# Narrow experts turn their activations by two half-width products, and experts two to eight are taken in another order

## The reference

```python
logits = einsum('bsd,de->bse', h, router_w) + router_b
top_vals, top_idx = lax.top_k(logits, 2)
top_w = softmax(top_vals)
combine = sum(one_hot(top_idx, 8) * top_w[..., None], axis=-2)
y = 0
for e in range(8):
    y = y + combine[..., e:e+1] * ((silu(h @ w_gate[e]) * (h @ w_up[e])) @ w_down[e])
x = x + gate_f * y
```

## Time and profile before

| | |
|---|---|
| median of three runs | 2416.67 us |
| lowest and highest | 2416.08, 2418.52 us |
| span of the profiled execution | 2415.4 us |
| TensorE busy | 2368.4 us, 98% of the span |
| VectorE busy | 935.5 us, 39% |
| ScalarE busy | 365.3 us, 15% |
| memory read | 614.69 MB |
| experts' stage, from the first expert's first product | 1464 us to the end |

### The profile page before, as it was taken

One profiled execution on the slowest core, in us unless ns is written; L12 is line 12 of the kernel. 1 busy time (PEld: TensorE's weight loads), 2 busy tenths in 40 slices (PEclk: granted clock), 3 DMA queues, 4 the chain that ended last, 5 costly groups with the idle time before them and its releaser, 6 DMA issues.

```text
span 2415.4 us, 30120 instructions
## 1 busy us (share of the span) xinstructions
PE 2368.4 (98%) x12002; PEld 1576.6 (65%) x12003; DVE 935.5 (39%) x1962; ACT 365.3 (15%) x988; POOL 55.4 (2%) x110
## 2 busy tenths in 40 slices
PE   9999999999999999999999999999999999999997
PEld 8956466669665666676788756699754445444553
DVE  4565233255564356755687462100211011101021
ACT  2254010012351100011000112100110010101111
POOL 0000000000000000000000000000000000000000
PEclk9999999999999999999999999999999999999999
DMA  7422343444322777454577469974999599958997
GB/s 277 149 111 97 113 173 141 152 177 167 128 81 94 270 297 299 194 194 192 227 302 308 167 247 394 424 289 186 375 422 419 206 381 421 425 231 358 417 426 295
DMA packets 78990, 617.61 MB, mean 256 GB/s; under 512 B 5984, under 2 KB 6112, under 8 KB 39184
## 3 DMA queue, kind: packets, MB, share of 16 engines
q1 hardware_dynamic: 73920, 558.39, 58.2%
q0 software_dynamic: 4656, 56.47, 5.6%
q10 hardware_dynamic: 288, 0.90, 0.1%
HBM read 614.69 MB, written 1.05 MB: 255 GB/s over the span
## 4 chain that ended last, share of the span: by engine, by line
PE 92%; DMA 4%; DVE 2%; ACT 1%; issue 1%; SPq 0%; POOL 0%; DVEq 0%; POOLq 0%; ACTq 0%
PE S L2972 9%; PE T L2592 9%; PE S L2974 8%; PE G L2331 6%; PE G L2608 5%; PE G L2986 4%; PE G L2988 4%; PE G L2363 3%; PE G L2546 3%; PE G L2871 3%; DMA big<-in_moe_pack 3%; PE S L2852 2%; PE G L2674 2%; PE T L3038 2%; PE G L2558 2%; PE G L3065 2%
## 5 line engine op out<-in xcount | busy, mean ns | idle before, releaser
L2186 DVE TENSOR_TENSOR turns<-S,turns 128x128 f32<-128x128 f32 (+2 forms) x105 | 35.5, 338 | 664.6 <-ACT turns L1280 664.6
L2972 PE MATMUL S<-big,hT 128*64 128x256 f32 x2240 | 272.1, 386 | 17.1 <-DMA big<-in_moe_pack 10.2
L2972 PEld LDWEIGHTS S<-big,hT 128*64 128x64 f32 x2240 | 157.1, 138 | 126.6 <-issue 44.2
L2592 PE MATMUL T<-hT,big 128*128 128x256 f32 x960 | 217.1, 379 | 1.1 <-ACT big L1168 1.1
L2592 PEld LDWEIGHTS T<-hT,big 128*128 128x128 f32 x960 | 182.1, 190 | 49.5 <-issue 27.7
L2974 PE MATMUL S<-big,hT 128*128 128x512 f32 x448 | 201.3, 593 | 0.3
L2974 PEld LDWEIGHTS S<-big,hT 128*128 128x128 f32 x448 | 82.8, 190 | 94.7 <-issue 94.7
L2363 PE MATMUL G<-big,hT 128*128 128x384 f32 x320 | 109.0, 490 | 0.8 <-ACT big L1058 0.8
L1285 ACT ACTIVATE pT<-T 128x128 f32<-128x128 f32 (+1 forms) x98 | 30.2, 308 | 518.9 <-PE T L2951 518.9
L2331 PE MATMUL G<-big 128*128 128x186 f32 (+1 forms) x536 | 91.8, 322 | 0.0
L2331 PEld LDWEIGHTS G<-big 128*128 128x128 f32 x536 | 86.6, 190 | 0.2
(11 more groups left out here) (500 smaller groups left out, 3494.6 us busy)
## 6 DMA issues: line engine op xcount, KB each, us to landing
big<-in_moe_pack SPq DMA_DIRECT2D x112, 2048.0 KB, 12.8
big<-in_moe_pack SPq DMA_DIRECT2D x72, 1024.0 KB, 10.0
big<-in_w_ff SPq DMA_DIRECT2D x32, 2048.0 KB, 8.0
big<-in_ada_pack POOLq DMA_DIRECT2D x24, 2048.0 KB, 12.2
big<-in_ffn_pack SPq DMA_DIRECT2D x11, 3072.0 KB, 12.7
big<-in_gate_pack SPq DMA_DIRECT2D x16, 1536.0 KB, 6.4
consts<-in_moe_pack SPq DMA_DIRECT2D x24, 1024.0 KB, 11.4
big<-in_proj_pack SPq DMA_DIRECT2D x15, 1488.0 KB, 6.4
```

The lines of the kernel that those rows point to most:

```text
L2592: ins = mm(up_bank(c, f), w[:, k, f * P:(f + 1) * P], hT[:, k, :], start=(k == 0), stop=(k == KD - 1))
L2972: ins = mm(S[s % 2][f * FEW:(f + 1) * FEW, 0:SEQ], hTe[:, k, 0:FEW], wt[:, k, f * SEQ:(f + 1) * SEQ], start=(k == 0), stop=(k == KD - 1))
```

## The change

`RANK_AT` becomes [0, 6, 0, 5, 1, 4, 2, 3]: after expert 0 come the fewest, the most, the second fewest, the second most and so on. Only the table changes; the code that each engine runs for a width stays where it is, and the table's row is an input.

In `turn_hidden` a narrow expert no longer transposes. It issues two ordinary products, each with 64 hidden channels of the activations as the stationary operand and the identity as the moving one, to PSUM partitions 0 to 63 and 64 to 127. The values land in the same places as before.

```diff
-RANK_AT = [0] + [(i - 1) // 2 if i % 2 else EXPERTS - 1 - i // 2 for i in range(1, EXPERTS)]
+RANK_AT = [0] + [TURNS - 1 - (i - 1) // 2 if i % 2 else i // 2 - 1 for i in range(1, EXPERTS)]
...
                     def turn_hidden(e, s, w):
 
                         pe.wait_ge(ehid_ok.sem, e * ESTEPS + (s + 3))
-                        for f in range(1 if few(w) else FT):
-                            ins = pe.transpose(T[0][:, s % 2 * SEQ + f * P:s % 2 * SEQ + (f + 1) * P], emsg[:, s % 2, SEQ + f * P:SEQ + (f + 1) * P], ident[:])
+                        for f in range(FT):
+                            if few(w):
+                                ins = mm(T[0][f * FEW:(f + 1) * FEW, s % 2 * SEQ:s % 2 * SEQ + P], emsg[:, s % 2, SEQ + f * FEW:SEQ + (f + 1) * FEW], ident[:], start=True, stop=True)
+                            else:
+                                ins = pe.transpose(T[0][:, s % 2 * SEQ + f * P:s % 2 * SEQ + (f + 1) * P], emsg[:, s % 2, SEQ + f * P:SEQ + (f + 1) * P], ident[:])
                         ins.then_inc(eh_turned.sem, 1)
```

## The result

| | before | changed |
|---|---|---|
| median, 20 runs each | 2418.8 us | 2424.2 us |
| lowest and highest | 2416.08, 2422.14 | 2418.64, 2431.19 |
| span of the profiled execution | 2415.4 | 2423.0 |

The ratio is 1.0023, with a 95% interval of 1.0017 to 1.0029: slower by 5.4 us, where 6.2 us less were forecast. The time lies 7 us above the end of the range, 2417.

The account below looks back on a forecast made before the run. TensorE, busy 98%, was taken as the bound, with DMA binding two neighbouring narrow experts. Terms -0.4 - 7.4 - 0.2 + 1.8 gave -6.2 us: span 2409.2, median 2410.5, range 2407 to 2417.

Parts of the forecast that it names:

- the order of the experts: Expert sequence: same seven width transitions, so the same pauses; the DMA-bound pair moves to turns 1 and 2; -0.4 us.
- The third: Rival: the 0.30 us around the transpose stay, turn 0.52 us, step from 5.64 us; +5.7 us, 2422.4; chance 0.10.
- The first rival's slower form: Turn's two halves don't run side by side, turn 0.44 us: +3.3 us, 2420.0; whole rival's chance 0.22.
- The turn within a step: Narrow experts: two products take 0.22 us where the transpose cost 0.41; 39 turns gain, -7.4 us; step 5.39 us.
- The turn of the last step: Between 128-wide gathers: 0.57 us with two switches instead of 0.11, +0.46 in four narrow experts, +1.8 us.
- A narrow expert followed by a narrow one: Narrow experts outside the DMA-bound pair: three, at -2.0 us each by the prediction's term.
- The DMA-bound pair: Two neighbouring narrow experts, moved from turns 7, 8 to 1, 2: stall 11.2 us against 10.2, at 425 GB/s.
- the 1650 named as the sign of a wrong term: Wide expert, forecast to start near 1647; a start beyond 1650 would make the order's term wrong.
- the first 12 pieces: Weights at the new pair's start: 18.9 MB in at 1464, leaving 69.2 MB to load from 1467.9 on.
- ScalarE's copy: Behind the turn, before `down`: slack of 0.31 us shrinks to about 0.1; the cover holds, but is thin.
- The order's -0.4: Term for the new expert order: last narrow expert done at 2405.8 against 2406.2; bounds +2.2 and -11.6 us.
- the late pair: Old order's two neighbouring narrow experts at turns 7 and 8, the last waiting 10.2 us for weights.

Follow-up runs that it names:

- before_pad84: Kernel before, plus 84 never-run instructions between TensorE's narrow and full bodies: 2432.61 us, ratio 1.0049 to the kernel before.
- order_only: Kernel before with only the new table of turns, the turn staying one transpose: 2420.09 us against 2419.77, ratio 0.9998.
- After_ahead128: Changed kernel plus 128 never-run instructions ahead of all TensorE expert code: 2400.83 us in one run; timed again 2403.63, ratio 0.9930 to the kernel before.

## Why the prediction was wrong

The step that failed is the one on the order of the experts: "So the 3.46 us in which TensorE waits for nothing shown between a full and a narrow expert, with the slow 5.36 and 5.26 us first group behind it ..., are paid twice in both". They are paid twice, but the price is 8.96 and 9.31, which is +11.35 us. I had counted the transitions and read their price as a property of the transition. It is one of where the code lies. That the code for each width stays where it is, as I wrote of the table, is true of the table alone: the two products make the narrow body longer and move the full body by 84 instructions. `before_pad84` shows the price with no change at all. No rival of mine had this either. The third, of a turn that keeps its 0.30 us, said 2422.4 and so comes nearest to 2424.2, by luck: its mark, a step of 5.64 or more, is absent, for the step is 5.39. The first rival's slower form, a turn of 0.44, is absent as well: the turn takes 0.22.

The other steps, by their own terms:

- The turn within a step was right: 0.22 us and 0.86 behind it. The saving is 0.19 us in 39 turns.
- The turn of the last step was right: 0.37 and 0.20 more behind it, the 0.57 that was forecast.
- A narrow expert followed by a narrow one takes 82.8 us in the changed kernel (84.9 with the old turn, in `order_only`), -2.0 as the sum had it.
- The DMA-bound pair: the wide expert starts at 1649.93, just below the 1650 named as the sign of a wrong term. Less the 3.8 us of the late start that is 1646.1, where 1647.1 was forecast; the stall is 11.4 us where 11 to 16 was expected, and the rate 425 GB/s, as taken. That the first 12 pieces are in at 1464 was slightly wrong: in the kernel before 266 GB/s still come from 1464 to 1468. The sum counts new loads from 1467.9 only, so nothing hangs on it.
- ScalarE's copy held its cover. TensorE's waits name it nowhere.
- The order's -0.4 held against the kernel before (`order_only`, 0.9998), but partly by luck: it rests on the pause in front of the late pair. With the pauses gone the order is worth 0.16% with the old turn and 0.30% with the new one. The first alone is within the uncertainty of two ratios, but its runs, taken side by side, hardly overlap (2405.97 to 2409.25 against 2409.14 to 2418.15).

The predicted span of 2409.2, with 11.35 for the pauses and 3.8 for the start, is 2424.4 against 2423.0 measured. The late start is read from one profiled execution of each kernel. The medians don't ask for it: -6.2 and 11.35 are +5.2, and they differ by 5.4.

What stays open is the rule. The Trainium skill, Runtime: NRT & Kernel Launch, Instruction fetch mechanics, says that instructions are refilled in 16 KB blocks of 256, with 128 KB for TensorE, and that a taken branch to a block outside the current window of two must wait for its read. The trace agrees with the size of the packets and with the wait: one or two of them begin within a pause from full to narrow. It doesn't agree with a window of two blocks. In the changed kernel's first expert, from 1467.9 to 1550.7, five packets come by the instruction queue q8; in the second, which runs the same body again, none. So at least those five blocks had been kept, and the measurement decides.

Which blocks are kept and when one is read ahead is not settled: neither the start places nor the distances alone foretell the waits of the table. Each body's branch back to the head carries a branch hint (`branch_hint(again)`), which may be what reads a block ahead; no run here takes it away. Nor does any run show what a block costs where the DMA isn't full. After_ahead128 is a lucky place found by trial, not one computed.

## What to carry to other kernels

Where the program branches between long bodies, an "issue" wait at a jump can be a price of where the code lies, as it was here: 0 to 10 us for the same work. An edit that makes one body longer can move it by several microseconds at each later jump, in either direction, so such an edit should be tried at two or three placements, or with the old code padded to the new length, before its own worth is judged. Look at the instruction queue in the DMA list at each change of body, both within the pause and in the 25 us ahead of it. And two narrow products among narrow ones are cheaper than a full-width transpose between them (0.22 against 0.41 us), but not between full-width neighbours (0.57 against 0.11).

## What the hardware showed that was not expected

Instructions arrive in packets of 16 KB, and while weights move at 420 GB/s a jump that waits for one costs several us: the pause with one read within was 3.46 us, the one with two 8.96, the reads 5 to 6 us apart. Both pauses also cost the clock, as above, and the first group of 32 records took 5.36 and 5.83 us against 3.60. 84 instructions that never ran cost 12.8 us (2432.61 against 2419.77); 128 that never ran, elsewhere, saved 7.4 (2412.49 against 2419.89).
